# Moving modulation tiles between the feed-forwards of a two-layer diffusion step, and two low parts of sums behind the last up pair

## The reference, cut to what matters

```python
ada = silu_c @ w_ada[l] + b_ada[l]                 # 9 x 1024 values for each layer and each of two vectors
s0, sc0, g0, s1, sc1, g1, s2, sc2, g2 = split(ada, 9)
n = rmsnorm(h, norm_g[l, 0]) * (1 + sc0) + s0
h = h + 0.5 * g0 * swiglu(n, w_ffn_up[l, 0], w_ffn_down[l, 0])   # d_ff 2816
n = rmsnorm(h, norm_g[l, 1]) * (1 + sc1) + s1
h = h + g1 * token_mix(n)
n = rmsnorm(h, norm_g[l, 2]) * (1 + sc2) + s2
h = h + 0.5 * g2 * swiglu(n, w_ffn_up[l, 1], w_ffn_down[l, 1])
```

## Time and profile before

| | us |
|---|---|
| runs | 3135.4, 3135.66, 3142.81 |
| median | 3135.66 |
| profiled execution, its own time | 3137.54 |
| span of its trace | 3135.4 |
| TensorE busy in the span | 3018.9 |
| VectorE busy | 2122.9 |

### The profile page before, as it was taken

How to read it: one execution, slowest core, us unless ns; L and a number is a source line. 1 busy time by engine, 2 the same in 40 slices (tenths; PEclk the granted TensorE clock), 3 DMA queues, 4 the chain that set the end, 5 groups by cost and what they waited for, 6 DMA issues and landing times.

```text
span 3135.4 us, 48664 instructions
## 1 busy us (share of the span) xinstructions
PE 3018.9 (96%) x19892; PEld 2938.2 (94%) x19892; DVE 2122.9 (68%) x3521; ACT 1141.8 (36%) x1820; POOL 85.8 (3%) x164
## 2 busy tenths in 40 slices
PE   7999999998999999999999999999899999999998
PEld 4899999997899999999999999999789999999998
DVE  7666666646655557988968988863565556785675
ACT  3422312422444433434343433442154443443432
POOL 0000000000000000000000000000000000000000
PEclk8999999999999999999999999999999999999999
DMA  8255553345122532444322434334521242122222
GB/s 304 91 202 228 213 190 135 115 153 221 67 75 85 192 112 80 135 141 142 122 95 94 149 121 142 108 114 163 224 82 71 76 186 108 68 95 81 95 68 75
DMA packets 89743, 408.90 MB, mean 130 GB/s; under 512 B 10049, under 2 KB 13569, under 8 KB 68914
## 3 DMA queue, kind: packets, MB, share of 16 engines
q1 hardware_dynamic: 60384, 285.76, 25.6%
q0 software_dynamic: 19872, 94.53, 8.3%
q10 hardware_dynamic: 9266, 25.50, 2.2%
HBM read 359.46 MB, written 46.30 MB: 129 GB/s over the span
## 4 chain that ended last, share of the span: by engine, by line
PE 77%; DVE 14%; ACT 4%; issue 3%; DMA 1%; ACTq 0%; DVEq 0%
PE tile_psum L743 21%; PE misc_psum L860 12%; PE tile_psum L750 11%; PE misc_psum L864 6%; PE tile_psum L1215 6%; PE tile_psum L704 3%; PE tile_psum L1219 3%; PE misc_psum L669 3%; PE tile_psum L669 2%; PE tile_psum L860 2%; PE tile_psum L709 2%; PE tile_psum L1080 1%; DVE h L2254 1%; DVE wlo L2083 1%; PE tile_psum L864 1%
## 5 line engine op out<-in xcount | busy, mean ns | idle before, releaser
L743 PE MATMUL tile_psum<-n_hi,whi 128*128 128x320 f32 x1536 | 352.3, 311 | 4.0 <-issue 2.2
L743 PE MATMUL tile_psum<-n_lo,whi 128*128 128x320 f32 x1536 | 350.1, 309 | 0.0
L2083 DVE TENSOR_TENSOR wlo<-raw,whi 128x2048 fp32r<-128x2048 f32 (+4 forms) x130 | 250.6, 1930 | 114.2 <-ACT whi L1491 112.2
L743 PE MATMUL tile_psum<-x_hi,whi 128*128 128x320 f32 x1300 | 300.1, 312 | 17.4 <-DVE h L2254 11.7
L743 PE MATMUL tile_psum<-x_lo,whi 128*128 128x320 f32 x1300 | 298.3, 311 | 0.0
L743 PEld LDWEIGHTS tile_psum<-n_hi,whi 128*128 128x128 f32 x1536 | 257.6, 189 | 6.8 <-DVE n_lo L2174 4.2
L743 PEld LDWEIGHTS tile_psum<-n_lo,whi 128*128 128x128 f32 x1536 | 258.2, 189 | 0.0
L1491 ACT ACTIVATE whi<-raw 128x2048 fp32r<-128x2048 f32 (+4 forms) x130 | 208.9, 1616 | 126.7 <-DMA raw<-in_w_down 43.7
L1215 PE MATMUL tile_psum<-n_hi,whi 128*128 128x320 f32 x768 | 237.4, 320 | 11.0 <-ACT gate_out L1978 10.3
L2254 DVE SCALAR_TENSOR_TENSOR h<-tile_psum,ada_t,h 128x320 f32<-128x320 f32 (+2 forms) x408 | 154.2, 434 | 129.2 <-PE tile_psum L750 127.5
L750 PE MATMUL tile_psum<-n_hi,wlo 128*128 128x320 f32 x1536 | 241.3, 309 | 0.0
(11 more groups left out here) (384 smaller groups left out, 6450.1 us busy)
## 6 DMA issues: line engine op xcount, KB each, us to landing
w_ada<-in_w_ada POOLq DMA_DIRECT2D x72, 512.0 KB, 4.0
raw<-in_w_up SPq DMA_DIRECT2D x72, 512.0 KB, 3.8
raw<-in_w_up SPq DMA_DIRECT2D x34, 1024.0 KB, 4.9
w_ada<-in_w_ada SPq DMA_DIRECT2D x56, 512.0 KB, 6.3
raw<-in_w_gate SPq DMA_DIRECT2D x24, 1024.0 KB, 4.9
raw<-in_w_down SPq DMA_DIRECT2D x29, 768.0 KB, 4.4
whi<-table_keep SPq DMA_DIRECT2D x20, 1024.0 KB, 4.7
wlo<-table_keep SPq DMA_DIRECT2D x20, 1024.0 KB, 6.9
```

The source lines that it names most:

```text
L743: pe.matmul(tps[:, t.s, m, 0:TH], blk(p, m * n + k)[0], (hi, lo)[b][:, k, tok], start=k == 0 and b == 0, stop=False)
L2083: ins = dve.tensor_tensor(lo_at(r, n)[:, 0:w], raw_at(r, n)[:, 0:w], hi_at(h_, n)[:, 0:w].bitcast(F32), ALU.subtract)
```

## The change

Three entries of the plan change, and `ADA_LATE` goes from 72 to 76 with the first. FF1 gets four more tiles: one more after each of the up panels 6 and 7 of the first chunk, and one more after each of the down panels 0 and 1 of its last chunk (2 instead of 1). FF2 and FF3 lose the tiles after up panels 2 and 3 and down panels 0, 1 and 3 of their first chunk (the one after down panel 2 stays); they get one more after up panel 0 of the last chunk (2 instead of 1), and one after each of the down panels 0 and 1 of the last chunk, where there was none. The number of tiles is the same. Four tile loads go from POOL's queue to SP's.

The low parts of sums 0 and 2 (`n_sum_low(0)`, `n_sum_low(2)`), which stood after the up pairs (2,1) and (3,0) of the first chunk of FF2, FF3 and FF4, both stand after (3,1).

```diff
-ADA_PLAN = {(0, 0): [0, 0, 2, 2, 2, 2, 1, 1] + [2] * 4 + [2] * 8 + [2] * 4 + [2] * 6 + [1, 1, 0, 0],
-            (0, 1): [0, 0, 1, 1] + [1] * 4 + [1] * 6 + [2, 2, 1, 1] + [1] * 6 + [2, 2, 1, 1] + [1] * 6 + [0] * 4,
-            (1, 0): [0, 0, 1, 1] + [1] * 4 + [1] * 6 + [2, 2, 1, 1] + [1] * 6 + [2, 2, 1, 1] + [1] * 6 + [0] * 4,
+ADA_PLAN = {(0, 0): [0, 0, 2, 2, 2, 2, 2, 2] + [2] * 4 + [2] * 8 + [2] * 4 + [2] * 6 + [2, 2, 0, 0],
+            (0, 1): [0] * 6 + [1, 0] + [1] * 6 + [2, 2, 1, 1] + [1] * 6 + [2, 2, 1, 1] + [2] + [1] * 5 + [1, 1, 0, 0],
+            (1, 0): [0] * 6 + [1, 0] + [1] * 6 + [2, 2, 1, 1] + [1] * 6 + [2, 2, 1, 1] + [2] + [1] * 5 + [1, 1, 0, 0],
             (1, 1): [0] * len(FAST_KINDS)}
...
                             if (i, j) == (2, 1):
                                 n_sum(1, [(sub, h11), (sub, l11)], sum_raw[0])
+                            if (i, j) == (3, 1):
                                 n_sum_low(0)
-                            if (i, j) == (3, 0):
                                 n_sum_low(2)
```

## The result

| us | before | after |
|---|---|---|
| median of eight runs each, same chip | 3138.28 | 3144.34 |
| lowest to highest | 3135.4 to 3143.1 | 3140.53 to 3149.47 |
| profiled execution, its own time | 3137.54 | 3143.12 |
| span of its trace | 3135.4 | 3141.3 |

A forecast was written before the change was run, and what follows sets the result against it. TensorE is busy 96% of the span, so order can win only 116 us, chiefly its waits on VectorE. Terms -9.2 + 2.8 + 2.5 + 3.4 + 3.9 + 0.4 = +3.8 us gave a median of 3139.5 us, range 3130 to 3146.

The forecast's parts named there:

- First chunks: First down panels of FF2 and FF3: fewer tiles gain 4.65 and 4.6 us; waits of 2.25 and 1.99 us remain.
- FF4: First chunk of FF4: moved low parts lengthen the wait at (1,1), losing 2.8 us, or 1.2 if the clock holds.
- FF1's tail: FF1's last down panels: two more tiles delay updates TensorE needs, +2.5 us, up to +4.1 with a second clock fall.
- FF2's and FF3's tails: Last down panels of FF2 and FF3: two new tiles each make TensorE wait, +3.4 and +3.9 us.
- Last chunk: Last chunk of FF2 and FF3: one more tile after up panel 0 costs 0.1 to 0.2 us each, +0.4 together.
- At nothing: FF1's two more tiles in up panels 6 and 7, and four loads moved to SP's queue, cost nothing.
- the tails are covered: Rival: tiles at the ends of FF1 to FF3 cost nothing; 3129.7 us, or 3124.6 with the clock holding; chance 0.14.
- VectorE late in the last chunk: Rival: VectorE's lateness stops TensorE at P7 of panels 1 to 5 in FF2 and FF3; 3147.1 us; chance 0.11.
- Every wait in the tails brings the low clock: Rival: clock falls add 1.6 us in FF1 and 1.2 each in FF2 and FF3; 3143.5 us; chance 0.13.

The follow-up runs named there:

- Experiments 1: Changed kernel with the low parts of sums 0 and 2 back behind up pairs (2,1) and (3,0), tile plan still changed; ratio 1.0005 to the kernel before.
- 2: Kernel before with only the low parts of sums 0 and 2 moved behind up pair (3,1), all tiles in their old places; ratio 1.0016 to the kernel before.
- 5: Changed kernel with the one tile of FF2's and FF3's first chunk behind down panel 3 instead of 2; ratio 1.0012 to the kernel before.
- the second trace: The changed kernel run and traced once more, nothing altered; FF4's first down panels lost 1.18 us instead of 2.55.
- Experiment 4: Changed kernel with FF2's and FF3's tail tile behind down panel 1 moved to up panel 4 of the second chunk; ratio 1.0025 to the kernel before.
- experiment 3: Changed kernel with the last down panels' tiles as before and six tiles moved into FF2's and FF3's fast chunks; ratio 0.9976 to the kernel before.

## Why the prediction was right, point by point

3139.5 us were forecast, 3144.34 measured: slower by less than 0.3%, as forecast. Of the 4.8 us between, 2.6 are the base: 3135.66 was the median of the first three runs, 3138.28 that of eight. The rest is 2.2 us: +3.8 forecast, +6.1 measured (6.18 by the parts). That the rest is so small is in part luck: in the traced execution the first chunks came out 1.9 us better than forecast, mostly because the clock held at one place, and the tails and what lies between 4.3 us worse.

- *First chunks*: -4.65 and -4.6 forecast, -6.28 and -4.58 measured. The waits are right to 0.02 us; FF2's clock held at (1,1), the spread that I had named. Experiments 1, 2 and 5 show each wait to be what I took it for, the low parts at (1,1) and the tile at (3,1).
- *FF4*: +2.8 forecast, +2.55 measured, 1.18 in the second trace without the fall: my two values, 1.2 and 2.8.
- *FF1's tail*: +2.5 forecast, +4.4 (4.8 in the second trace) measured. This term was mis-sized. The token sums are 4.0 us later, as forecast, but in the prediction I let the clock fall at (1,1), "held until 562.0 and then likely on the low clock", and so let that fall take the wait at the token sums. The clock held there, the token sums waited 1.38 us, and the fall came behind them, as it had before the change. I also left out the second half's token sums, which wait 0.4 us more (0.8 in the second trace). My upper value of 4.1 had a second fall and not this order.
- *FF2's and FF3's tails*: +3.4 and +3.9 forecast, +3.83 and +4.71 measured. Waits of 1.1 and 1.5 us were forecast, 1.03 and 1.38 measured; I gave each tail 0.5 us for a fall by chance, and in both traces of the kernel after it came in each. Net, it cost 0.75 and 1.06 us there (3.83 against 3.08, 4.71 against 3.65 where the clock held). Experiment 4 shows the split between the two tiles.
- *Last chunk*: +0.4 forecast for the two together; measured +0.38 in FF2 and, with the section closing there, +0.87 in FF3. Another 0.53 in FF2's middle down panels (a wait of 1.18 us for 0.64 at 1481.62) was not in the sum: a section of eight closes ahead of that update now, since fewer tiles stand before it.
- *At nothing*: FF1's extra tiles in up panels 6 and 7, right (0.10 us more, 0.34 less in the second trace). One reading of the earlier trace rows was loose: slices 21 and 27 of VectorE are at 6 tenths, not at 8 or 9; nothing hangs on it.
- *Rivals*: "the tails are covered" is refuted by experiment 3. "VectorE late in the last chunk" asked for a wait over 1 us at P7 of panel 1; it was 0.15 and 0.76. "Every wait in the tails brings the low clock" is half right: not every wait, but each tail once in both traces of the kernel after, and not in all of the other kernels with the same waits (the tails of 3.08 and 3.65 us in the table are without it). Its 3143.5 us came nearer to the measured time than my own. The Trainium skill, "TensorE: Matmul & The Clock Gate", under HAM oscillation, says that the return to the full clock is paid again at each fall; the three tails agree, 0.72 each time. That every wait here would bring a fall was my reading, not the page's words, and the runs are against it: 1.00 in the 6 us behind the 1.99 us at 1270.05.

## What to carry to other kernels

Price an instruction that is moved in an in-order queue against the next thing that another engine takes from that queue, inside the one pair or panel where it stands; idle time averaged over a longer stretch promised room that three tiles in one pair did not have. Work that is taken from a bad place must be priced where it lands: in the traced execution the first chunks won 11 us, and the tails lost 13. Where three parts of a change pull apart, keep them apart: without the tail tiles and the moved low parts, and with the one tile a panel later, the same idea was worth 14 us as timed.

## What I had not expected of the hardware

- Equal waits do not bring equal clocks. Of 21 waits of 2.26 to 2.28 us at pair (1,1) in the traces of these kernels, the clock fell behind 7 (0.72 to 0.74 over the next 6 us): 0 of 5 in FF1 and 0 of 5 in FF2, 3 of 5 in FF3, 4 of 6 in FF4. Yet behind the 1.38 us at FF1's token sums, some 5 us after one of them, it fell in all five. Place counts as well as length; what decides is not settled here.
- A fall need not cost its 1.7 us where a wait on VectorE follows soon: in one trace without it the next wait grew from 2.36 to 3.88 us.
